# Second-stack layer: the order of its first stage and of its attention loop

## What is computed

```python
h = rms_norm_2(x, g_pre_mix)
u, q, k, v, iq, ik, iw = split(h @ w_in)
q, k = rope(q), rope(k); iq, ik = rope(iq), rope(ik)
a = pool_mixer(u, w_pool, pool_scale)       # sliding means over 2, 4, 8, 16 tokens, then a small product
logits = einsum('bqhd,bsd->bqhs', iq, ik) * 64 ** -0.5
score = einsum('bqh,bqhs->bqs', iw, relu(logits))
score = where(allowed, score, -inf)
top_val, top_idx = top_k(score, topk)       # only these keys take part
s = einsum('bqhd,bqkhd->bqhk', q, k[top_idx]) * 64 ** -0.5
o = einsum('bqhk,bqkhd->bqhd', softmax(s), v[top_idx])
x = x + rms_norm_2(concatenate([a, o]) @ w_out, g_post_mix)
x = x + rms_norm_2(relu(rms_norm_2(x, g_pre_ffn) @ w_ff1) ** 2 @ w_ff2, g_post_ffn)
```

## Time and profile before

| | |
|---|---|
| median of 3 runs | 2473.79 us (2472.6 to 2477.57) |
| the profiled execution | 2474.91 us |
| its span, first to last instruction | 2473.1 us |
| TensorE busy | 2401.5 us, 97% |
| VectorE busy | 1360.4 us, 55% |
| ScalarE busy | 896.2 us, 36% |
| GpSimd busy | 349.4 us, 14% |
| mean granted TensorE clock | 0.991 |

### The profile page before, as it was taken

One profiled execution on the slowest core, in us unless ns is written; L12 is line 12 of the kernel. 1 busy time (PEld: TensorE's weight loads), 2 busy tenths in 40 slices (PEclk: granted clock), 3 DMA queues, 4 the chain that ended last, 5 costly groups with the idle time before them and its releaser, 6 DMA issues.

```text
span 2473.1 us, 28917 instructions
## 1 busy us (share of the span) xinstructions
PE 2401.5 (97%) x11498; PEld 1942.6 (79%) x11498; DVE 1360.4 (55%) x1976; ACT 896.2 (36%) x1295; POOL 349.4 (14%) x270
## 2 busy tenths in 40 slices
PE   8999999999999999999999999999999999999997
PEld 6877888888787788888876778888886777888886
DVE  7775443345786543334569866334356975633433
ACT  4555332234455523223433354223242244422331
POOL 2002000002200200000347411000013732000002
PEclk9999999999999999999999999999999999999998
DMA  4311222222321222222221121222221211122221
GB/s 156 109 54 69 102 86 102 102 85 95 108 94 52 73 102 102 89 98 88 100 90 69 69 73 52 102 102 88 99 102 56 86 52 69 68 102 102 85 102 51
DMA packets 33180, 215.56 MB, mean 87 GB/s; under 512 B 4144, under 2 KB 4400, under 8 KB 8112
## 3 DMA queue, kind: packets, MB, share of 16 engines
q1 hardware_dynamic: 33072, 214.08, 24.2%
HBM read 211.97 MB, written 2.10 MB: 87 GB/s over the span
## 4 chain that ended last, share of the span: by engine, by line
PE 83%; DVE 8%; ACT 3%; POOL 3%; issue 2%; DMA 0%; SPq 0%; POOLq 0%; DVEq 0%; ACTq 0%
PE ps L415 77%; DVE wl L366 1%; POOL wl L396 1%; PE ps L2187 1%; DVE gl L639 1%; ACT wh L360 1%; PE ps L2201 1%; PE ps L2211 1%; PE ps L1380 1%; DVE arena L1897 1%; PE ps L1404 1%; PE ps L309 1%; PE ps L597 1%; PE ps L1367 1%; POOL arena L1647 0%
## 5 line engine op out<-in xcount | busy, mean ns | idle before, releaser
L415 PE MATMUL ps<-gh,wh 128*128 128x512 f32 x1488 | 590.0, 397 | 15.1 <-DVE gl L639 11.4
L415 PE MATMUL ps<-hh,wh 128*128 128x512 f32 x1456 | 576.5, 396 | 5.6 <-DVE arena L1861 2.5
L415 PE MATMUL ps<-gh,wl 128*128 128x512 f32 x1488 | 580.7, 390 | 0.0
L415 PE MATMUL ps<-gl,wh 128*128 128x512 f32 x1488 | 580.7, 390 | 0.0
L415 PE MATMUL ps<-hh,wl 128*128 128x512 f32 x1456 | 568.2, 390 | 0.0
L415 PE MATMUL ps<-hl,wh 128*128 128x512 f32 x1456 | 568.1, 390 | 0.0
L360 ACT ACTIVATE wh<-wr 128x2048 fp32r<-128x2048 f32 x188 | 358.7, 1908 | 556.2 <-PE ps L415 556.0
L366 DVE TENSOR_TENSOR wl<-wr,wh 128x2048 fp32r<-128x2048 f32 x168 | 387.9, 2309 | 278.2 <-ACT wh L360 275.9
L415 PEld LDWEIGHTS ps<-gh,wh 128*128 128x128 f32 x1488 | 279.5, 188 | 83.8 <-DVE gl L639 13.9
L415 PEld LDWEIGHTS ps<-hh,wh 128*128 128x128 f32 x1456 | 273.6, 188 | 71.3 <-issue 11.2
L415 PEld LDWEIGHTS ps<-gh,wl 128*128 128x128 f32 x1488 | 279.3, 188 | 60.0
(11 more groups left out here) (260 smaller groups left out, 2444.4 us busy)
## 6 DMA issues: line engine op xcount, KB each, us to landing
wr<-in_weights SPq DMA_DIRECT2D x195, 1024.0 KB, 4.8
out_yt<-x SPq DMA_DIRECT2D x8, 256.0 KB, 2.0
x<-in_xt SPq DMA_DIRECT2D x3, 512.0 KB, 8.3
wr<-in_weights SPq DMA_DIRECT2D x2, 512.0 KB, 6.2
arena<-in_gates SPq DMA_DIRECT2D x2, 512.0 KB, 8.0
arena<-in_embed SPq DMA_DIRECT2D x2, 512.0 KB, 5.4
par<-in_params_b SPq DMA_DIRECT2D x2, 274.0 KB, 2.8
x<-in_xt SPq DMA_DIRECT2D x2, 256.0 KB, 4.3
```

The source lines that it names most:

```text
L415: done = pe.matmul(out, stationary, moving, start=(first and n == 0), stop=(last and n == 2), skip_group_check=True)
```

## The change

Both second-stack layers are changed, in six points.

- Roots. Folded: `normed_sums` follows `sum_squares` directly, before chunk 1, and `spreads` comes after slice 1 of it instead of slice 5. Other layer: `sum_squares` stands before the last slice of the paired chunks, and `spreads` after it, before chunk 2.
- The weights' turn and the logits begin in the first tile of chunk 3 (slice 2 folded, slice 4 otherwise). ScalarE's split of chunk 5 comes after the twelve logits, VectorE's drains of `u` come later, and its split of chunk 3 after the four first rotations.
- ScalarE splits chunk 10 before it takes the last pooled product.
- The last round of picks replaces and masks one query tile after the other, the longest first, and signals each.
- Two half tiles of the pooled product run before the first scores (in bank 7), two after the second; in the loop steps 2, 6, 10 and 14 have none.
- Within a pair of heads the longest query tile comes first (i = 3 - s % 4). The scores of the first four steps wait for their own mask. The splits within the loop move to steps 2 and 10, the products for x to steps 6 to 13.

The diff, without the lines that only carry the new order of query tiles a second time:

```diff
@@ -434,7 +434,7 @@
-def first_two_chunks(pe, mem, sem, c0, tile, before, sums, spreads, more_sums=None):
+def first_two_chunks(pe, mem, sem, c0, tile, before, sums, spreads, spread_at=KT - 3):
@@ -460,10 +460,8 @@
     for k in range(KT):
-        if k == 2 and more_sums:
-            more_sums()
         part(k, 1)
-        if k == KT - 3:
+        if k == spread_at:
             spreads()
@@ -1531,6 +1529,11 @@
+POOLED_BANKS = (7,) + (0,) * (KT - 1)
+POOLED_STEPS = [s for s in range(QT * HEADS2 // 2) if s % QT != 2]
+POOLED_AFTER = [None, 0] + [s + 1 for s in POOLED_STEPS[1::2]]
...
 def b_bank(tile):
@@ -1714,15 +1717,17 @@
                            scale=DH ** -0.5).then_inc(sem["rectified"], 1)
-            if s == 4:
-                split_high(act, mem, sem, 5)
+        split_high(act, mem, sem, 5)
         split_high(act, mem, sem, 6)
...
         for g in range(4):
+            if g == 3:
+                split_high(act, mem, sem, 7 + g)
             act.wait_ge(sem["pool_product"], g + 1)
...
                            scale=par[:, BP_SCALE + g:BP_SCALE + g + 1]).then_inc(sem["pool_high"], 1)
-            split_high(act, mem, sem, 7 + g)
+            if g < 3:
+                split_high(act, mem, sem, 7 + g)
         act.wait_ge(sem["drained"], B_TILE[B_V])
@@ -1733,7 +1738,7 @@
         def exponents(s):
-            n, b = P * (s % QT + 1), s % 2
+            n, b = P * (QT - s % QT), s % 2
             act.wait_ge(sem["maxed"], s + 1)
@@ -1761,9 +1766,9 @@
             untangle(s)
-            if s == 0:
+            if s == 2:
                 split_high(act, mem, sem, B_POOL + 1)
-            if s == STEPS // 2:
+            if s == STEPS // 2 + 2:
                 split_high(act, mem, sem, B_ATT)
@@ -1865,8 +1870,8 @@
             rotate_first(t, t, iq[:, t, :], sem["index_rotated"], sem["index_swapped"])
-            if folded and t == 1:
-                split_low(dve, mem, sem, 3)
+        if folded:
+            split_low(dve, mem, sem, 3)
         rotate_first(4, 4, ik, sem["index_rotated"], sem["index_swapped"])
@@ -1879,14 +1884,13 @@
         dve.wait_ge(sem["padded"], 1)
-        drain_u(6)
         dve.wait_ge(sem["weights_turned"], 1)
...
             n, out = P * (i + 1), score[:, i - 1, 0:P * (i + 1)]
-            if s in (5, 10):
-                drain_u(7 + s // 10)
+            if s == 6:
+                drain_u(6)
             dve.wait_ge(sem["rectified"], s + 1)
@@ -1897,6 +1901,7 @@
+        drain_u(7)
         dve.wait_ge(sem["weighed"], 2 * len(LOGITS))
@@ -1921,8 +1926,9 @@
         picks(1)
+        drain_u(8)
+        picks(1)
         drain_u(9)
-        picks(1)
@@ -1940,16 +1946,26 @@
         pool_low(3)
-        picks(TOPK // 8 - rounds[0])
-        own.mark(dve.tensor_copy(mask[0], cst[:, C_CHUNK:C_CHUNK + P]))
+        picks(TOPK // 8 - 1 - rounds[0])
         own.settle()
-        for i in range(1, QT):
+        for i in reversed(range(1, QT)):
+            own.mark(dve.max(top[:, i - 1, :], score[:, i - 1, 0:P * (i + 1)]))
+        found = own.count
...
+        def last_picked(i):
             n = P * (i + 1)
+            own.mark(dve.match_replace(out=score[:, i - 1, 0:n], in_to_replace=top[:, i - 1, :], in_values=score[:, i - 1, 0:n], imm_value=MARK))
+            own.settle()
             dve.tensor_scalar(mask[i], score[:, i - 1, 0:n], 0.9 * MARK, NEG, ALU.is_gt, ALU.mult)\
...
+        for i in reversed(range(1, QT)):
+            dve.wait_ge(sem["own"], found - i + 1)
+            last_picked(i)
+        dve.tensor_copy(mask[0], cst[:, C_CHUNK:C_CHUNK + P]).then_inc(sem["masked"], 1)
...
         def maxima(s):
-            n, b = P * (s % QT + 1), s % 2
+            n, b = P * (QT - s % QT), s % 2
             two = slice(SM_MAX + 2 * b, SM_MAX + 2 * b + 2)
@@ -1974,20 +1990,24 @@
         def keep_pooled(n):
+            if n == 0:
+                dve.wait_ge(sem["drained"], B_TILE[B_POOL])
             dve.wait_ge(sem["product"], B_TILE[B_POOL] + n + 1)
-            dve.tensor_copy(branch(n), ps[:, 0, :]).then_inc(sem["drained"], 1)
+            dve.tensor_copy(branch(n), ps[:, POOLED_BANKS[n], :]).then_inc(sem["drained"], 1)
...
         maxima(1)
-        dve.wait_ge(sem["masked"], QT - 1)
+        dve.wait_ge(sem["masked"], QT)
+        keep_pooled(0)
         for s in range(STEPS):
             scale_rows(s)
-            if s and s % 2 == 0:
-                keep_pooled(s // 2 - 1)
+            if s in POOLED_AFTER:
+                keep_pooled(POOLED_AFTER.index(s))
             if s > QT and s % QT == 1:
                 pair_low(s // QT - 1)
-            if folded and s < KT:
-                dve.scalar_tensor_tensor(out=x[:, s, :], in0=x[:, s, :], scalar=cst[:, C_GFIN + s:C_GFIN + s + 1], in1=raw_root,
+            if folded and s >= STEPS - KT - 2 and s < STEPS - 2:
+                k = s - (STEPS - KT - 2)
+                dve.scalar_tensor_tensor(out=x[:, k, :], in0=x[:, k, :], scalar=cst[:, C_GFIN + k:C_GFIN + k + 1], in1=raw_root,
                                          op0=ALU.mult, op1=ALU.mult).then_inc(sem["renewed"], 1)
@@ -2115,20 +2135,24 @@
-        def sums_within(k):
-            if k == 2:
+        def both_sums():
+            sum_squares(pe, mem, sem, 0)
+            normed_sums()
...
+        def last_slice_and_sums(k):
+            gained(0)(k)
+            if k == KT - 1:
                 sum_squares(pe, mem, sem, 0)
...
         if folded:
-            first_two_chunks(pe, mem, sem, 0, 0, gained(0), lambda: sum_squares(pe, mem, sem, 0), spreads, normed_sums)
+            first_two_chunks(pe, mem, sem, 0, 0, gained(0), both_sums, spreads, 1)
             product_tile(pe, mem, sem, B_IKW, 0, 4, mem.gh, mem.gl, bank=b_bank(4))
         else:
-            paired_chunks(pe, mem, sem, 0, 0, gained(0))
-            product_tile(pe, mem, sem, B_IKW, 0, 4, mem.gh, mem.gl, before=sums_within, bank=b_bank(4))
+            paired_chunks(pe, mem, sem, 0, 0, last_slice_and_sums)
             spreads()
+            product_tile(pe, mem, sem, B_IKW, 0, 4, mem.gh, mem.gl, bank=b_bank(4))
         product_tile(pe, mem, sem, B_IKW, P, 5, mem.gh, mem.gl, width=HEADS2, bank=b_bank(5))
-        product_tile(pe, mem, sem, 3, 0, B_TILE[3], mem.gh, mem.gl)
@@ -2150,14 +2174,21 @@
-        def weights_and_logits(k):
-            if k == 2:
-                turn_weights()
-            if k >= 4:
-                logits(k - 4)
...
-        product_tile(pe, mem, sem, 3, P, B_TILE[3] + 1, mem.gh, mem.gl, before=weights_and_logits)
-        product_tile(pe, mem, sem, 4, 0, B_TILE[4], mem.gh, mem.gl, before=lambda k: logits(4 + k))
+        turned_at = 2 if folded else 4
...
+        def weights_and_logits(first):
...
+            def at(k):
+                slot = first + k - turned_at
+                if slot == 0:
+                    turn_weights()
+                elif 0 < slot <= len(LOGITS):
+                    logits(slot - 1)
+            return at
...
+        product_tile(pe, mem, sem, 3, 0, B_TILE[3], mem.gh, mem.gl, before=weights_and_logits(0))
+        product_tile(pe, mem, sem, 3, P, B_TILE[3] + 1, mem.gh, mem.gl, before=weights_and_logits(KT))
+        product_tile(pe, mem, sem, 4, 0, B_TILE[4], mem.gh, mem.gl, before=weights_and_logits(2 * KT))
         product_tile(pe, mem, sem, 4, P, B_TILE[4] + 1, mem.gh, mem.gl)
@@ -2178,8 +2209,10 @@
         def scores(s):
-            j, i = divmod(s, QT)
+            j, i = s // QT, QT - 1 - s % QT
             n, b = P * (i + 1), s % 2
+            if s < QT:
+                pe.wait_ge(sem["masked"], s + 1)
             if s >= 2:
@@ -2202,9 +2235,9 @@
         def weigh(s):
-            j, i = divmod(s, QT)
+            j, i = s // QT, QT - 1 - s % QT
             pe.wait_ge(sem["untangled"], s + 1)
-            if i == 0 and j:
+            if s % QT == 0 and j:
                 pe.wait_ge(sem["pair_low"], j)
@@ -2221,26 +2254,31 @@
-        def pooled_part(s):
-            n, part = divmod(s, 2)
+        def pooled_part(p):
...
+            n, part = divmod(p, 2)
             c = B_POOL + n // 4
-            if s % 8 == 0:
+            if p % 8 == 0:
                 pe.wait_ge(sem["low"], split_count(c))
-            if part == 0:
+            if n >= 2 and part == 0:
                 pe.wait_ge(sem["drained"], B_TILE[B_POOL] + n)
-            half_tile(c, n % 4, 0, (2 * part, 2 * part + 1), 0, part == 1)
...
+            half_tile(c, n % 4, POOLED_BANKS[n], (2 * part, 2 * part + 1), 0, part == 1)
...
+        pe.wait_ge(sem["pool_low"], 4)
+        pooled_part(0)
+        pooled_part(1)
         pe.wait_ge(sem["drained"], B_TILE[B_POOL])
-        pe.wait_ge(sem["masked"], QT - 1)
         pe.wait_ge(sem["rotated"], 8)
-        pe.wait_ge(sem["pool_low"], 4)
         scores(0)
         scores(1)
+        pooled_part(2)
+        pooled_part(3)
         for s in range(STEPS):
...
             turn(s)
-            pooled_part(s)
+            if s in POOLED_STEPS:
```

(1 more changed line is left out.)

## The result

| | before | changed |
|---|---|---|
| median of six runs, us | 2474.73 (2472.60 to 2477.57) | 2461.75 (2454.31 to 2465.74) |
| profiled execution, us | 2474.91 (span 2473.1) | 2454.31 (span 2452.5) |
| its mean granted clock | 0.991 | 0.996 |

The ratio is 0.9945, 95% interval 0.9935 to 0.9955: 13.0 us faster, where 27.6 were forecast for the median and 26.7 between profiled executions. The profiled executions are 20.6 us apart; the changed one was the quickest of its six runs, and the other five took 2460 to 2466 us. So there are two gaps to explain: from 26.7 to 20.6, and from 20.6 to 13.

The account below looks back on a forecast made before the run. TensorE, busy 97% of the span, was taken to bound the kernel. Gains of 12.4 us (first layer) and 14.3 (second), together 26.7, took 2474.91 to 2448.2; less 1.1 for the runs' median, 2447.1 us, range 2440 to 2459.

Parts of the forecast that it names:

- the gain of 1.3 us: First layer's roots: 16 small matmuls move into TensorE's 1.14 us gap before the second chunk, gaining 1.3 us.
- The wait for rectified logits: TensorE's 0.9 us wait late in the logits stage, forecast to go in both layers with logits a tile earlier.
- the wait forecast there at 0.9 us: Second layer's logits: TensorE's second logit waits 0.9 us for a weighing slowed by GpSimd's split, bounds 0.1 to 1.4.
- VectorE's chain to the mask: VectorE's picks, rounds and rotations move up; the last round by 2.2 us, first mask ready at 1392.7 us.
- Second layer's roots: Root spread some 5.8 us sooner, so the 2.5 us rotation wait and its 1.65 us clock drop go: 4.1 us.
- 1.9 + 1.65 = 3.6 us in each layer: Value tiles: TensorE's 1.9 us wait for GpSimd's split and the 1.65 us clock drop behind it both go.
- a wait of 1.0 us forecast: Before the first scores TensorE waits 1.0 us for the first mask, bounds 0 and 2.5, in place of 1.7.
- I charge one per split: Loop: each GpSimd split stretches one scaling, giving two 0.6 us waits, 1.2 us a layer, without a drop.
- The row on which I leaned: Trace of the loop at 1440.48 us: first scaling stretched to 1.32 us, the second its usual 0.41.
- the first rival: Both scalings of two long tiles a layer stretched, waits of 1.4 us with drops, 9.8 us lost: 2457; chance 0.15.
- I count every wait of 1.5 us and more with its drop: Clock: each such TensorE wait is followed by 3.3 us at half clock, costing 1.65 us, which goes with it.
- None below 1.2 us with one: Clock: no TensorE wait shorter than 1.2 us was counted with a drop to half clock behind it.

Follow-up runs that it names:

- e13_roots_back: Changed kernel with the first layer's small matmuls on normed squares and the spreads put back where they were; median 2463.61 us, +0.4 us at the same clock.
- e10_value_split_back: Changed kernel with ScalarE again splitting the last value chunk behind the last pooled product; median 2463.18 us, +0.6 us at the same clock.
- e6_splits_in_idle: Changed kernel with ScalarE doing both loop splits before the evacuation of the transposes, not behind it; median 2470.85 us, +3.7 us at the same clock.
- e8_masks_and_splits: e6_splits_in_idle plus the last two pick rounds tile by tile, an earlier first maximum and ScalarE emptying pooled tile 0; median 2465.19 us.
- e11_shortest_first: Changed kernel with query tiles shortest first again in loop and masks, splits at the first and ninth step; median 2476.74 us, +10.2 us at the same clock.

## Why the forecast was wrong

*Front of the first layer: the waits right, the gain of 1.3 us too high.* The small matmuls run from 1255.75 us, in the gap, and the second chunk starts at 1257.53. But e13_roots_back, which undoes this, loses only 0.4 to 0.6 us, with an error of 0.5; the new row of small matmuls mostly has a longer fall of the clock about it, and its cost stood in no term. The wait for rectified logits is gone. One of 0.8 us for a weighing (L2173 for L1898) is left; the kernel before had 1.2 us at the same place (L2149 for L1894, at 1295 us), which the forecast did not read. In the second layer the wait forecast there at 0.9 us is 1.0 long. VectorE's chain to the mask, which decides, was on time all the same.

*Second layer's roots: right.* The 2.5 us are gone, and 0.5 us for the last rotation (L2161) is what is late next.

*The value split: the wait went as said, the gain did not come.* The step that failed is "1.9 + 1.65 = 3.6 us in each layer". I had computed that VectorE sets the first mask at 1392.7 us (1392.9 measured), and what sets a time behind a wait swallows the wait: e10_value_split_back puts 1.9 us back in each layer and costs 0.6 in all at the same clock, 0.1 in the layer without a fall. The 1.65 for a fall was not all nothing: in the layer where one came, it cost 1.6.

*The first mask: a wait of 1.0 us forecast, 2.0 measured.* Most of it is no loss: TensorE's pooled matmuls end at 1390.9 us, 0.8 sooner than computed, and the mask is ready at 1392.9, 0.2 later. The first scores start 0.4 us later than forecast in the first layer, and 1.1 in the second.

*The loop: "I charge one per split" failed.* Both scalings are blocked, the wait is 1.5 us instead of 0.6, at all four places. The rule of the Trainium skill, "SBUF — State Buffer", section "SBUF: two separate sides", that the forecast set against the row was right; e6_splits_in_idle showed it in its pure form. The Trainium skill says in the section "Who interferes with whom" of "SBUF — State Buffer" that a reduction never contends and that a tensor-scalar operation can; the maxima (1.23 us beside GpSimd, 1.22 alone) and the scalings above agree. The row on which I leaned, 1.32 and then 0.41 us, was the end of a GpSimd run: its four pieces lie from 1436.60 to 1441.58 us, and the second scaling starts at 1441.72.

The four waits are 0.9 us longer each, 3.6 us; the first scores account for 0.4 + 1.1, the rest of the two loops for 1.0: 6.1 us, from 26.7 to the 20.6 between the profiles. The mechanism of the first rival happened, without its falls in that execution.

*The clock: "I count every wait of 1.5 us and more with its drop" is the step that cost most.* A drop of 1.65 us is right in size (1.6). But the seven drops that I booked as the change's were those of one execution. Two of them (in the value tiles) cost nothing, and the other five, 8.0 us, are in most executions of the changed kernel made up by as many elsewhere, at places as far off as the first stack; that rests on its two profiles and on the mean clocks of its runs. 26.7 - 6.1 - 8.0 = 12.6; the median moved by 13.0, the table above gives 12.4, the line through all runs 11.6. "None below 1.2 us with one" fell too: the stretches at 1259 and 1485 us follow no long wait, but begin among small matmuls.

Open stays why a fall comes in one execution and not in the next. Behind the 2.0 us for the mask it came in 12 of 18 places, behind the waits of 1.5 us in the loop in 2 of 22. The longer waits for scaled rows in e6_splits_in_idle, e8_masks_and_splits and e11_shortest_first, 1.9 to 3.0 us, had one in 10 of 13 places; so within the loop too the longer waits have it more often. What else differs between the places was not tried.

## What to carry to other kernels

Before booking a fall of the clock as a saving, take a second profile: its cost belongs to the execution until it shows at the same place again. Compare kernels at equal mean clock to see what the waits are worth, and by their medians as well, since an edit that makes waits of 2 us or more brings falls of its own. A wait removed ahead of a point that another engine sets is worth nothing as long as slack is left there. Where GpSimd must work beside VectorE's operations between SBUF tiles, cut its instructions small: each such operation here took about as long as one whole GpSimd instruction, so many short VectorE operations beside long pieces are the worst pairing.

## What the hardware showed that was not expected

- A scaling of 128 columns beside GpSimd takes nearly as long as one of 512 (1.18 and 1.30 us against 1.31 and 1.48), with pieces of 1.2 to 1.3 us; beside pieces of 0.76 us one of 512 takes 0.90 and 0.94, beside 0.46 us 0.50 and 0.67. Even a 128x2 operation went from 0.17 to 0.72.
- A granted clock of 0.50 for 6.8 us, from within the last 16 of 32 small matmuls that follow a wait of 0.7 us and six full ones (128x512), in 12 of 15 profiles.
- A granted clock of 0.50 behind waits of TensorE of 1.5 us in the loop at 2 of 22 places, behind 2.0 us for the mask at 12 of 18, behind 1.9 to 3.0 us in the loop at 10 of 13.
- Eleven runs of one kernel lie between 2454 us (mean clock 0.996) and 2467 us (0.990), the longer the lower their clock.
